# One transformer-like block on a Trainium2 core: small work of VectorE and GpSimd exchanged, S5 inputs in another order, norm sums and reload moved

## The chip, the cores and the metric

The kernel runs on one core of a Trainium2 chip. The metric is the device time of one execution in microseconds, median of several runs. A core has TensorE (matrix products, PE in the profile, its weight loads as PEld), VectorE (DVE), ScalarE (ACT), GpSimd (POOL) and SyncE (SP), which here issues nearly all DMAs. TensorE's clock is granted at one of two levels, 1.2 or 2.4 GHz; the profile gives the granted share as PEclk.

## The reference, cut to what matters

One layer of a hybrid encoder over 2048 prompt tokens and 8 sequences of 16 sample tokens, width 1024, in float32.

```python
h = rmsnorm(x, g);  u = h @ W_in                     # 2828 columns for four head groups
y_a = RG-LRU(conv(u_x)) * gelu(gate)                 # linear recurrence
y_b = SSD(x, B, C, softplus(dt_raw + bias), a)       # chunked state space scan, gated norm
y_c = gated delta rule(l2norm(q), l2norm(k), v, g, beta)
y_d = S5(u_d): complex diagonal states, associative scan, gelu, glu
x += concat(y_a, y_b, y_c, y_d) @ W_out
x += softmax(rmsnorm(x) @ W_q @ K^T / 16) @ V @ W_o  # 256 memory tokens, 4 heads
h = rmsnorm(x);  x += (silu(h @ W_g) * (h @ W_u)) @ W_d   # 2816 hidden columns
y = rmsnorm(x)
```

The states at the end of each recurrence and the memory keys and values are outputs too.

## The kernel before

**Dense work.** Every float32 operand of a dense product is held as two halves, a rounded one (hi) and the rest (lo), and `three` (lines 441 to 443) issues three matmuls for one product. A weight block of 128 x 1024 comes from HBM as `raw`; ScalarE makes its hi half (line 856), VectorE its lo half (line 1040); for blocks that later passes need again, SyncE stores both halves in `kept_dram` (`sp_keep`), and later passes load the halves instead (`sp_kept`, two transfers of 512 KB). There are RAWS 3 raw buffers and SPLITS 4 buffers for the halves. A buffer can be written again when TensorE has used it and its store has landed (`slot_free`). `SPLIT_AHEAD, LOAD_AHEAD, KEPT_AHEAD = 2, 4, 2` (line 36) say how many blocks ahead of its use a block is split, its raw form is loaded, its kept halves are loaded.

**Passes and sections.** Tokens run in six passes of 2, 3, 3, 3, 3 and 3 tiles of 128. All dense work is one ordered list of 787 sections, `SECS`: in a pass `u` and `z` (W_in), `w` (W_out), then attention (`s`, `pt`, `vo` and others), `g`, `up` and `d` (feed-forward), `st` (the sums of squares over the partitions, TensorE line 749) and `final` (scaling and storing the output). The dense results use three PSUM banks in turn. The `st` and the four `final` sections of pass p lie inside the W_in stage of pass p+2, since one pass's mixer overlaps the dense work of another: `st` stands behind the tenth `u` section (`units[9]`). Its input is the running sum `acc` that VectorE builds from ScalarE's squares (line 1049).

**The mixer.** Each of the 17 tiles is a chunk of 21 steps (25 for the sample tile). A generator per engine runs the mixer (`pe_mixer`, `act_mixer`, `dve_mixer`, `pool_mixer`), and `weave` (line 2637) fixes each engine's instruction order: section i, then PLAN[i] steps of the mixer. The plan starts with 16 setup steps and has four steps of token scalars (`dve_scalars`: softplus of dt and of a, on [128, 8 x tiles]) in front of each pass's chunks. An engine works strictly in its order, so a wait holds all that stands behind it.

**Who does what before.** VectorE: lo halves, evictions, convolution taps (line 1131), setup (`dve_setup`, lines 2369 to 2488: exponent, sine arguments, the matrices `bb`, the rotations `rot`), token scalars, scans (line 2073). GpSimd: gate x `rstd` of the feed-forward (line 1270, for every `g` section, 132 times), and in each chunk eight row scalings of the mask `L` (lines 2509 and 2515), three maskings (2520, 2522, 2527) and x times D (2533). TensorE transposes `bb` at setup step 14 (line 1770) and computes the S5 inputs with `pe_bu` (line 1493). SyncE reloads `x` for the next pass in one transfer of 1.5 MB at `u` section 16, once the outputs of the pass before are stored.

Of the kernel before, what the change touches and what calls it, by code (L numbers as in the profile page):

```python
# [14 lines left out]
P = 128  # L15
# [20 lines left out]
SPLIT_AHEAD, LOAD_AHEAD, KEPT_AHEAD = 2, 4, 2  # L36
# [98 lines left out]
def schedule():  # L135
# [108 lines left out]
    for p in range(NP):  # L244
# [20 lines left out]
        if a:  # L265

            units = [s for s in a if s.kind == "u"]
            for k in range(KD):
                units[1 + k].squares = [(fin, k)]
            at = a.index(units[9]) + 1  # L270
            a[at:at] = [st]
            for e, u in zip(end, units[10:]):
                at = a.index(u) + 1
                a[at:at] = [e]
        else:
            for s in last:
                s.squares = [(fin, 2 * s.b), (fin, 2 * s.b + 1)]
            a = [st] + end
# [212 lines left out]
def program(nc, t):  # L491
    ctx = ExitStack()
    with ctx:
# [122 lines left out]
        gs_done, up_done = sem("gs_done"), sem("up_done")  # L616
        out_ready, out_stored = sem("out_ready"), sem("out_stored")
# [518 lines left out]
        def dve_second(eng, i):  # L1136
# [9 lines left out]
            elif unit is not None and unit.cv >= 0:  # L1146
                dve_taps(eng, unit)
            elif s.kind == "up":
# [4 lines left out]
            elif s.kind == "pt":  # L1153
                wide = prompt_at(s.p)[1] * P
                for mt in range(2):
                    slot = s.a % 2 * 2 + mt
                    eng.wait_ge(g_hi_done, s.g + mt + 1)
                    eng.tensor_tensor(g_lo[:, slot, 0:wide], banks[:, (s.f + mt) % 3, 0:wide],
                                      g_hi[:, slot, 0:wide].bitcast(F32), ALU.subtract).then_inc(g_lo_done, 1)
                    eng.drain().then_inc(free[(s.f + mt) % 3], 1)  # L1160
# [26 lines left out]
        def dve_section(eng, i):  # L1187
# [16 lines left out]
            if s.kind == "z" and s.a == 0:  # L1204
                for j in range(tiles(s.p)):
# [4 lines left out]
            elif s.kind == "w":  # L1210
                if s.a == 0:
                    eng.wait_ge(x_loaded, 16 * (s.p + 1))
# [4 lines left out]
            elif scores_at(i) is not None:  # L1217
                s = scores_at(i)
                for j in score_tiles(s):
# [6 lines left out]
                                             ALU.mult).then_inc(s_max, 1)  # L1226
            elif s.kind in ("vo", "so", "d"):
# [22 lines left out]
            elif s.kind == "up":  # L1250
                eng.wait_ge(gs_done, HID * s.p + s.a + 1)
# [10 lines left out]

        def pool_section(eng, i):
            unit = evicted_at(i)
            if unit is not None and unit.kind == "g":
                g = gs[:, unit.a % 2, 0:cols(unit.p)]
                eng.wait_ge(g_gated, unit.ev + 1)
                eng.tensor_tensor(g, g, rstd[:, unit.ni % 2, 0:cols(unit.p)], ALU.mult).then_inc(gs_done, 1)  # L1270
# [103 lines left out]
        def sp_section(eng, i):  # L1374
# [55 lines left out]
            lg=2, dec_m=2, xsd=1)  # L1430
        per_chunk = {k: v if isinstance(v, tuple) else (v, v) for k, v in per_chunk.items()}
        ms = {k: sem("m_" + k) for k in list(per_chunk) + ["in_q", "in_x", "in_l", "in_z", "y_l", "y_x", "y_s", "y_g"]}
        tok_pe, tok_act, tok_dve, tok_exp = sem("tok_pe"), sem("tok_act"), sem("tok_dve"), sem("tok_exp")
        setup_act, setup_dve, setup_pe = sem("setup_act"), sem("setup_dve"), sem("setup_pe")
        state_done = sem("state_done")

        class Chunk:


            def __init__(self, eng, p, c):  # L1440
# [4 lines left out]
                self.ts = tsc[:, p % 2, self.tile, :]  # L1445

# [295 lines left out]
        def pe_scalars(eng, p):  # L1742
# [5 lines left out]
            eng.wait_ge(tok_dve, 2 * p + 2)  # L1748
# [33 lines left out]

        def act_chunk(eng, k):

            k.need("turn", 1)
# [8 lines left out]
            k.need("dec_g")  # L1794
            eng.activation(m["dec"], banks[:, 3, :], ACT.Exp).then_inc(ms["dec_x"], 1)
# [139 lines left out]
        def act_mixer(eng):  # L1935
            for n in range(N_SETUP):
# [41 lines left out]
        def dve_scalars(eng, p):  # L1978
# [7 lines left out]
            eng.scalar_tensor_tensor(na, x8, -1.0, x8, ALU.mult, ALU.min)  # L1986
            eng.drain().then_inc(tok_dve, 1)
# [15 lines left out]
            eng.scalar_tensor_tensor(sp, x8, 0.0, a, ALU.max, ALU.add)  # L2003
# [12 lines left out]
            eng.drain().then_inc(tok_dve, 1)  # L2016
            yield
# [845 lines left out]
```

## Time and profile before

| what | value |
|---|---|
| median of 3 runs | 4240.63 us (4239.75 to 4242.36) |
| the profiled execution | 4238.34 us, of it 4236.5 us span |
| TensorE busy | 3748.2 us, 88% of the span |
| VectorE, ScalarE, GpSimd busy | 2228.1, 1255.2, 320.8 us |
| mean granted TensorE clock | 0.927 |
| DMA | 942 MB, mean 222 GB/s |

How to read it: TensorE is the busiest engine, so what counts is its idle time, 488.3 us in sum, and time at the lower clock. Other engines matter where TensorE waits for them. In the section of rows, a line of a window gives start and end, the length, busy time with the number of instructions for PE, PEld, DVE, ACT and POOL, then PEclk, the DMA share and GB/s. A line of waits gives who waited, for whom, the sum, how often, and the longest. The stages of a pass stand behind each other: W_in (139 us), W_out (37), attention (109) and feed-forward (367) in a middle pass.

### The profile page before, as it was taken

Reading aid. Unit: us, or ns where it says so; the run is one execution under the profiler, and the core shown is the slowest. Engines: PE = TensorE matmul, PEld = TensorE weight load, DVE = VectorE, ACT = ScalarE, POOL = GpSimd, SP = SyncE. Lnnn points to the kernel's source line nnn. Section 1 sums busy time; section 2 is a strip of 40 time slices with the busy share of each in tenths; the row PEclk is TensorE's granted clock in tenths of the full one; section 3 lists DMA queues with packets and bytes.
Section 4 is the critical chain, followed back from the end, with each engine's and each line's share of the span. In section 5 each row is a group of like instructions: output and inputs, shape, how many; then the busy total and the mean of one; then the engine's idle time right before and its main releaser. Section 6 shows DMA issues by size and latency. Waiting matters only on the chain.

```text
span 4236.5 us, 63633 instructions
## 1 busy us (share of the span) xinstructions
PE 3748.2 (88%) x24250; PEld 3627.6 (86%) x24250; DVE 2228.1 (53%) x4752; ACT 1255.2 (30%) x2291; POOL 320.8 (8%) x340
## 2 busy tenths in 40 slices
PE   5587868898788899997899997899998899998998
PEld 5586867798788899997899997899998799998998
DVE  7576644167773545563555554554455455543323
ACT  4344332145432322222323232323232322322101
POOL 0010000001100001100101100001010001100000
PEclk8798977689999999998999998999999999999999
DMA  7755585479968456567555666556666655566776
GB/s 246 239 170 175 175 299 209 130 266 364 350 247 275 163 195 220 206 219 251 191 195 210 220 221 220 208 197 210 212 223 221 216 177 206 199 212 246 244 251 216
DMA packets 372574, 942.08 MB, mean 222 GB/s; under 512 B 35120, under 2 KB 168752, under 8 KB 371760
## 3 DMA queue, kind: packets, MB, share of 16 engines
q1 hardware_dynamic: 372272, 938.03, 63.6%
q8 instruction: 193, 3.16, 0.3%
q14 instruction: 109, 0.89, 0.1%
HBM read 763.32 MB, written 174.57 MB: 221 GB/s over the span
## 4 chain that ended last, share of the span: by engine, by line
PE 54%; DVE 16%; DMA 11%; PEld 6%; DVEq 4%; ACT 3%; issue 3%; SPq 2%; ACTq 0%; PEldq 0%
PE banks L441 15%; PE banks L442 14%; PE banks L443 14%; DMA uc_dram<-uc_sb 3%; DVE m_p_sb L2073 2%; DMA kept_dram<-wlo_sb 2%; DMA wlo_sb<-kept_dram 2%; PEld banks L443 2%; DVE uc_sb L1131 2%; PEld banks L441 2%; PEld banks L442 2%; PE banks L1512 1%; PE banks L1518 1%; DVE wlo_sb L1040 1%; PE banks L1521 1%
## 5 line engine op out<-in xcount | busy, mean ns | idle before, releaser
L441 PE MATMUL banks<-hh_sb,whi_sb 128*128 128x384 f32 (+2 forms) x3552 | 1216.0, 342 | 162.2 <-DVE wlo_sb L1040 58.1
L442 PE MATMUL banks<-hh_sb,wlo_sb 128*128 128x384 f32 (+2 forms) x3552 | 1181.8, 333 | 0.0
L443 PE MATMUL banks<-hl_sb,whi_sb 128*128 128x384 f32 (+2 forms) x3552 | 1180.2, 332 | 0.0
L441 PEld LDWEIGHTS banks<-hh_sb,whi_sb 128*128 128x128 f32 x3552 | 696.6, 196 | 193.1 <-issue 69.1
L442 PEld LDWEIGHTS banks<-hh_sb,wlo_sb 128*128 128x128 f32 x3552 | 697.1, 196 | 2.1 <-issue 1.2
L443 PEld LDWEIGHTS banks<-hl_sb,whi_sb 128*128 128x128 f32 x3552 | 696.0, 196 | 0.0
L441 PE MATMUL banks<-g_hi_sb,whi_sb 128*128 128x384 f32 (+2 forms) x1568 | 541.9, 346 | 77.6 <-DVE g_lo_sb L1151 30.1
L442 PE MATMUL banks<-g_hi_sb,wlo_sb 128*128 128x384 f32 (+2 forms) x1568 | 528.4, 337 | 0.0
L443 PE MATMUL banks<-g_lo_sb,whi_sb 128*128 128x384 f32 (+2 forms) x1568 | 528.3, 337 | 0.0
L441 PEld LDWEIGHTS banks<-g_hi_sb,whi_sb 128*128 128x128 f32 x1568 | 316.5, 202 | 91.2 <-DVE g_lo_sb L1151 33.3
L1232 DVE TENSOR_TENSOR x_sb<-x_sb,banks 128x384 f32<-128x384 f32 (+2 forms) x400 | 202.4, 514 | 330.9 <-PE banks L443 327.4
L441 PE MATMUL banks<-whi_sb,hh_sb 128*128 128x256 f32 (+1 forms) x784 | 246.2, 314 | 108.5 <-DVEq L1160 37.9
L442 PEld LDWEIGHTS banks<-g_hi_sb,wlo_sb 128*128 128x128 f32 x1568 | 317.3, 202 | 0.0
L443 PEld LDWEIGHTS banks<-g_lo_sb,whi_sb 128*128 128x128 f32 x1568 | 316.5, 202 | 0.0
L1023 ACT ACTIVATE g_hi_sb<-gf_sb 128x384 fp32r<-128x384 f32 (+1 forms) x132 | 66.9, 507 | 724.8 <-DVE gf_sb L1253 724.6
L1040 DVE TENSOR_TENSOR wlo_sb<-raw_sb,whi_sb 128x1024 fp32r<-128x1024 f32 (+1 forms) x162 | 199.6, 1235 | 152.4 <-ACT whi_sb L856 150.8
L1270 POOL TENSOR_TENSOR gs_sb<-gs_sb,rstd_sb 128x384 f32<-128x384 f32 (+1 forms) x132 | 129.4, 980 | 1947.9 <-ACT gs_sb L906 1947.9
L441 PEld LDWEIGHTS banks<-whi_sb,hh_sb 128*128 128x128 f32 x784 | 166.3, 212 | 117.9 <-DVEq L1160 39.6
L442 PE MATMUL banks<-whi_sb,hl_sb 128*128 128x256 f32 (+1 forms) x784 | 237.8, 303 | 0.0
L443 PE MATMUL banks<-wlo_sb,hh_sb 128*128 128x256 f32 (+1 forms) x784 | 237.0, 302 | 0.0
L1253 DVE TENSOR_TENSOR gf_sb<-gs_sb,banks 128x384 f32<-128x384 f32 (+1 forms) x132 | 69.8, 529 | 302.4 <-PE banks L443 289.8
L856 ACT ACTIVATE whi_sb<-raw_sb 128x1024 fp32r<-128x1024 f32 (+1 forms) x162 | 169.4, 1051 | 76.0 <-DMA kept_dram<-wlo_sb 62.8
(411 smaller groups left out, 5143.7 us busy)
## 6 DMA issues: line engine op xcount, KB each, us to landing
whi_sb<-kept_dram SPq DMA_DIRECT2D x560, 512.0 KB, 3.7
wlo_sb<-kept_dram SPq DMA_DIRECT2D x560, 512.0 KB, 4.8
raw_sb<-w SPq DMA_DIRECT2D x144, 512.0 KB, 5.0
kept_dram<-whi_sb SPq DMA_DIRECT2D x112, 512.0 KB, 6.5
kept_dram<-wlo_sb SPq DMA_DIRECT2D x112, 512.0 KB, 7.3
uc_dram<-uc_sb SPq DMA_DIRECT2D x90, 192.0 KB, 3.4
ldb_sb<-x_t SPq DMA_DIRECT2D x72, 192.0 KB, 4.6
x_sb<-x_t SPq DMA_DIRECT2D x5, 1536.0 KB, 9.2
```

Of the source, the lines that this page charges most:

```text
L441: eng.matmul(out, xh, yh, start=first, stop=False)
L442: eng.matmul(out, xl, yh, start=False, stop=False)
L443: return eng.matmul(out, xh, yl, start=False, stop=last)
L856: eng.activation(whi[n % SPLITS][:, 0:width], raw[m % RAWS][:, 0:width], ACT.Copy).then_inc(w_hi_done, 1)
L1023: eng.activation(g_hi[:, s.a - sum(BLOCKS[:s.b]), 0:n], gf[:, s.a % 2, 0:n], ACT.Copy).then_inc(g_hi_done, 1)
L1040: eng.tensor_tensor(wlo[n % SPLITS][:, 0:width], raw[m % RAWS][:, 0:width], whi[n % SPLITS][:, 0:width].bitcast(F32), ALU.subtract).then_i ...
L1131: last = eng.scalar_tensor_tensor(out[:, 0:n], u[:, tap:tap + n], wc, out[:, 0:n], ALU.mult, ALU.add)
L1232: eng.tensor_tensor(out, out, bank[:, 0:wide], ALU.add).then_inc(free[(s.f + dd) % 3], 1)
L1253: eng.tensor_tensor(gf[:, s.a % 2, 0:n], gs[:, s.a % 2, 0:n], bank[:, 0:n], ALU.mult).then_inc(up_done, 1)
L1270: eng.tensor_tensor(g, g, rstd[:, unit.ni % 2, 0:cols(unit.p)], ALU.mult).then_inc(gs_done, 1)
L1512: last = eng.matmul(banks[:, 3, h * P:h * P + P], head("decs", h, P), head("ST1", h, P), start=True, stop=True)
L2073: eng.tensor_tensor_scan(dst[:, s * P:s * P + P], mag[:, n:n + 1].to_broadcast([P, P]), src[:, s * P:s * P + P], s5_x[:, part, n:n + 1], A ...
```

## The change

- Setup and the whole token softplus run on GpSimd alone, without being woven in (`setup`, `scalars`); only reciprocals stay on VectorE. Operations with three operands are written as two. `yield`s fall away. The other engines wait for `setup_pool` counts; SyncE, ScalarE and VectorE wait for 5, the end of the setup, before the first chunk.
- The gate x `rstd` product goes to VectorE, the mask rows to ScalarE (`act_rows`, eight per chunk), the maskings and x times D to VectorE. The strict mask falls away.
- `pe_bu` issues the two halves of the partitions in turn instead of one after the other.
- `st` stands two `u` sections later, and each `final` as well.
- VectorE evicts `pt` after its squares and taps; PLAN is 0 at these sections.
- `x` is reloaded in quarters at `u` 16, `u` 17, `z` 0 and `z` 1.
- SPLIT_AHEAD goes from 2 to 3 and LOAD_AHEAD from 4 to 5.

```diff
-SPLIT_AHEAD, LOAD_AHEAD, KEPT_AHEAD = 2, 4, 2
+SPLIT_AHEAD, LOAD_AHEAD, KEPT_AHEAD = 3, 5, 2
...
-            at = a.index(units[9]) + 1
+            at = a.index(units[11]) + 1
             a[at:at] = [st]
-            for e, u in zip(end, units[10:]):
+            for e, u in zip(end, units[12:]):
...
+            elif unit is not None and unit.kind == "g":
+                g = gs[:, unit.a % 2, 0:n]
+                eng.wait_ge(g_gated, unit.ev + 1)
+                eng.tensor_tensor(g, g, rstd[:, unit.ni % 2, 0:n], ALU.mult)
+                eng.drain()
...
             elif s.kind == "up":
-                eng.wait_ge(gs_done, HID * s.p + s.a + 1)
...
-            if s.kind == "u" and s.b == 16 and s.p >= 2:
-                sp_x(eng, s.p - 1)
+            if s.p >= 2 and (s.kind == "u" and s.b >= 16 or s.kind == "z"):
+                sp_x(eng, s.p - 1, s.b - 16 if s.kind == "u" else 2 + s.a)
...
-            for half, bank in enumerate((bank_a, bank_b)):
-                r = slice(half * 64, half * 64 + 64)
-                for part in range(2):
-                    for u in range(2):
-                        o = part * 256 + u * P
+            for part in range(2):
+                for u in range(2):
+                    o = part * 256 + u * P
+                    for half, bank in enumerate((bank_a, bank_b)):
+                        r = slice(half * 64, half * 64 + 64)
                         eng.matmul(banks[:, bank, o:o + P], bbt[r, part, j, u, :], in_l[r, 4 + j, :], start=True, stop=True)
...
                 if n == N_SETUP - 2:
-                    eng.wait_ge(setup_dve, 3)
+                    eng.wait_ge(setup_pool, 4)
...
+        def act_rows(eng, k, first):
+            for h in range(4):
+                eng.activation(lg[:, h, :], k.later, ACT.Copy, scale=k.ts[:, G8 + first + h:G8 + first + h + 1])
+            eng.drain().then_inc(ms["lg"], 1)
         def act_chunk(eng, k):
+            k.before("ws")
+            act_rows(eng, k, 4)
             k.need("turn", 1)
...
             k.need("dec_g")
+            act_rows(eng, k, 0)
             eng.activation(m["dec"], banks[:, 3, :], ACT.Exp).then_inc(ms["dec_x"], 1)
...
-            tt(by_pair(m["decs"]), kq[:, 0], by_pair(m["decs"]), ALU.mult)
-            tt(by_pair(m["dec"]), kq[:, 1], by_pair(m["dec"]), ALU.mult)
+            tt(by_pair(m["decs"]), kq[:, 0], by_pair(m["dec"]), ALU.mult)
...
+            tt(by_pair(m["dec"]), kq[:, 1], by_pair(m["dec"]), ALU.mult)
...
+            tt(m["xsd"], m["tx"][:, 0:256], mc("ssd_d"), ALU.mult)
+            tt(dec, dec, k.upto.unsqueeze(1).to_broadcast([P, 4, P]), ALU.mult)
+            k.need("dec_x", 2)
+            tt(dcs, dcs, k.upto.unsqueeze(1).to_broadcast([P, 4, P]), ALU.mult)
...
         def dve_mixer(eng):
-            yield from dve_setup(eng)
-            for p in range(NP):
-                yield from dve_scalars(eng, p)
-                if p == 0:
-                    eng.wait_ge(sample_in, 16 * 4)
-                yield from chunks(eng, p, dve_chunk)
+            for n in range(N_SETUP):
+                if n == 3:
+                    eng.wait_ge(setup_pool, 3)
+                    eng.reciprocal(sw[8][:], sw[8][:])
+                    eng.reciprocal(sm[:, 6:8], sm[:, 6:8])
+                    eng.drain().then_inc(setup_inv, 1)
+                yield
+            for p in range(NP):
+                yield
+                eng.wait_ge(tok_den, p + 1)
+                z = tk[:, 5, 0:tiles(p) * 8]
+                eng.reciprocal(z, z).then_inc(tok_inv, 1)
+                yield
+                yield
+                eng.wait_ge(tok_exp, p + 1)
+                yield
+                if p == 0:
+                    eng.wait_ge(setup_pool, 5)
+                    eng.wait_ge(sample_in, 16 * 4)
+                yield from chunks(eng, p, dve_chunk)
...
         def pool_mixer(eng):
-            for _ in range(N_SETUP):
-                yield
+            for _ in setup(eng):
+                pass
+            eng.drain().then_inc(setup_pool, 1)
             for p in range(NP):
+                eng.wait_ge(r12_done, PASSES[p][1])
+                if p:
+                    eng.wait_ge(tok_pe, p)
+                    eng.wait_ge(ms["upd"], PASSES[p - 1][0])
+                scalars(eng, p)
```

## Rows read from the trace of the kernel before

**Rows 1.** The page: busy us by engine; stores of kept halves
```profile
PE 3748.2 (88%) x24250; PEld 3627.6 (86%) x24250; DVE 2228.1 (53%) x4752; ACT 1255.2 (30%) x2291; POOL 320.8 (8%) x340
...
kept_dram<-wlo_sb SPq DMA_DIRECT2D x112, 512.0 KB, 7.3
```

**Rows 2.** By window: us, then busy (x) of PE, PEld, DVE, ACT, POOL
```profile
19.00:166.00 147.00, 94.21 (x550) 88.62 (x550) 105.20 (x369) 61.29 (x105) 0.00 (x0) 0.83 0.75 247
592.00:878.00 286.00, 236.68 (x1284) 210.88 (x1285) 105.19 (x218) 73.27 (x136) 9.06 (x8) 0.67 0.54 185
878.00:1197.00 319.00, 267.61 (x2188) 259.65 (x2188) 229.57 (x398) 151.35 (x226) 39.09 (x46) 0.94 0.93 347
1854.00:1993.00 139.00, 117.58 (x731) 114.17 (x731) 75.27 (x162) 40.22 (x72) 0.00 (x0) 0.93 0.69 236
2139.00:2506.00 367.00, 355.92 (x2276) 349.56 (x2275) 187.30 (x361) 93.14 (x171) 44.32 (x46) 0.98 0.60 207
3940.00:4237.00 297.00, 279.96 (x1592) 277.73 (x1590) 79.35 (x137) 34.38 (x61) 22.30 (x22) 0.97 0.69 237
```

**Rows 3.** Waits: engine, line <- releaser: total us, times, longest
```profile
ACT whi_sb L856 <- DMA kept_dram<-wlo_sb: 62.8, 31, 6.7
...
PE banks L441 <- DVE wlo_sb L1040: 67.2, 24, 7.2
PE banks L441 <- DMA wlo_sb<-kept_dram: 52.1, 21, 6.6
DVE uc_sb L1095 <- DMA uc_dram<-uc_sb: 88.5, 19, 8.0
PE banks L749 <- DVE acc_sb L1049: 33.0, 6, 7.2
```

**Rows 4.** Timeline: start, us, engine, line, operation, shape, count
```profile
123.44 1.91 PE L1770 MATMUL banks<-mixc_sb,bb_sb 128*128 128x128 f32 x16
```

**Rows 5.** By shape: count | busy, mean ns; DVE until 165 us
```profile
L1270 POOL TENSOR_TENSOR gs_sb<-gs_sb,rstd_sb 128x384 f32<-128x384 f32 x110 | 112.6, 1024 | 1563.4 <-ACT gs_sb L906 1563.4
L2509 POOL TENSOR_SCALAR m_lg_sb<-mixc_sb,tsc_sb 128x128 f32<-128x128 f32 x64 | 40.6, 653 | 1004.4 <-DVEq L2016 931.0 <-PE banks L1483 73.4
L2856 POOL MEMSET const-float32-0.0<- 128x1 f32 x1 | 0.1, 99 | 0.2 <-issue 0.2
...
L2358 DVE TENSOR_TENSOR ex_sb<-ex_sb 128x8 f32<-128x8 f32 x16 | 2.7, 167 | 1.2
L2463 DVE TENSOR_TENSOR bt_sb<-sw_sb,s5b_sb 128x1024 f32<-128x1024 f32 x1 | 1.2, 1221 | 0.0
...
L1846 ACT ACTIVATE m_yo_sb<-banks,tsc_sb 128x64 f32<-128x64 f32 x68 | 15.8, 315 | 53.9 <-PE banks L1612 53.5 <-PE banks L1483 0.5
```

**Rows 6.** Chain by line, 880 to 1190 us, then 1850 to 1960
```profile
by line: DMA kept_dram<-wlo_sb 12.0%; PE banks L441 7.9%; PE banks L443 7.1%; PE banks L442 7.0%; ACT whi_sb L856 6.4%; DVE wlo_sb L1040 6.4%; DVEq L1254 4.9%; DVE m_p_sb L2073 4.5%; issue 4.4%; DVEq L1089 3.2%; DMA ldb_sb<-x_t 2.7%; DVE m_
...
by line: DMA uc_dram<-uc_sb 17.9%; DVE uc_sb L1131 12.3%; DMA wlo_sb<-kept_dram 4.9%; PE banks L441 4.8%; PE banks L442 4.3%; PE banks L443 4.3%; issue 4.0%; DVE acc_sb L1049 3.1%; ACT uc_sb L924 2.6%; DVE m_p_sb L2073 2.5%; PEld banks L442
```

**Rows 7.** Timeline around the norm sums L749, [idle before <- releaser]
```profile
1905.68 0.34 PE L443 MATMUL banks<-hl_sb,whi_sb 128*128 128x384 f32 x1
1912.49 1.65 PE L749 MATMUL banks<-acc_sb,ones_sb 128*128 128x384 f32 x2 [6.48 <-DVE acc_sb L1049]
...
1911.88 0.56 DVE L1049 TENSOR_TENSOR acc_sb<-acc_sb,sqb_sb 128x384 f32<-128x384 f32 x1
...
1967.46 0.59 PE L441 MATMUL banks<-whi_sb,hh_sb 128*128 128x268 f32 x1 [4.76 <-DMA wlo_sb<-kept_dram]
```

**Rows 8.** timeline of 1600 to 1612 us: DVE, GpSimd, TensorE
```profile
1602.71 5.11 DVE L2073 TENSOR_TENSOR_SCAN m_p_sb<-mag_sb,s_x_sb,m_p_sb 128x128 f32<-128x128 f32 x8
...
1601.03 3.62 POOL L2515 TENSOR_SCALAR m_lg_sb<-mixc_sb,tsc_sb 128x128 f32<-128x128 f32 x4
...
1604.47 0.34 PE L443 MATMUL banks<-g_lo_sb,whi_sb 128*128 128x384 f32 x1
1608.32 0.69 PE L441 MATMUL banks<-g_hi_sb,whi_sb 128*128 128x384 f32 x1 [3.52 <-DVE x_sb L1232]
1608.81 0.52 PE L442 MATMUL banks<-g_hi_sb,wlo_sb 128*128 128x384 f32 x1
```

**Rows 9.** timeline, the same scans with GpSimd idle
```profile
1888.85 3.12 DVE L2073 TENSOR_TENSOR_SCAN m_p_sb<-mag_sb,s_x_sb,m_p_sb 128x128 f32<-128x128 f32 x8
```

**Rows 10.** timeline, two blocks of 16 matmuls with 64 rows in each operand
```profile
1591.24 1.71 PE L1493 MATMUL banks<-m_in_l_sb,bbt_sb 64*128 64x128 f32 x16
...
243.15 1.16 PE L1564 MATMUL banks<-m_cht_sb 64*128 64x128 f32 x16 [0.28 <-ACT m_cht_sb L1800]
```

More of the change, by code:

```diff
@@ L615, in program @@
         s_max, s_exp, p_done = sem("s_max"), sem("s_exp"), sem("p_done")
-        gs_done, up_done = sem("gs_done"), sem("up_done")
-        out_ready, out_stored = sem("out_ready"), sem("out_stored")
+        up_done = sem("up_done")
+        out_ready, out_stored = sem("out_ready"), [sem(f"out_stored{q}") for q in range(KD // 2)]
         qs_done, ps_done, pst_done = sem("qs_done"), sem("ps_done"), sem("pst_done")
@@ L1152, in dve_second @@
                                   ALU.subtract).then_inc(g_lo_done, 1)
[L1153 to L1160, printed above, removed]
             elif s.kind == "sv":
@@ L1226, in dve_section @@
                                              ALU.mult).then_inc(s_max, 1)
+            elif s.kind == "pt":
+                wide = prompt_at(s.p)[1] * P
+                for mt in range(2):
+                    slot = s.a % 2 * 2 + mt
+                    eng.wait_ge(g_hi_done, s.g + mt + 1)
+                    eng.tensor_tensor(g_lo[:, slot, 0:wide], banks[:, (s.f + mt) % 3, 0:wide],
+                                      g_hi[:, slot, 0:wide].bitcast(F32), ALU.subtract).then_inc(g_lo_done, 1)
+                    eng.drain().then_inc(free[(s.f + mt) % 3], 1)
             elif s.kind in ("vo", "so", "d"):
@@ L1445, in __init__ @@
                 self.ts = tsc[:, p % 2, self.tile, :]
+                self.upto = sc("Us") if self.sample else mc("U")
+                self.later = sc("Ls") if self.sample else mc("L")
             def base(self, name):
@@ L2002, in dve_scalars @@
             eng.drain()
-            eng.scalar_tensor_tensor(sp, x8, 0.0, a, ALU.max, ALU.add)
+            eng.tensor_scalar(sp, sp, 0.5, None, ALU.mult)
+            eng.drain()
+            eng.tensor_tensor(sp, sp, a, ALU.add)
             eng.drain()
@@ L2173, in dve_chunk @@
             k.need("kq")
-            k.need("dec_m", 1)
+            k.need("dec_x", 1)
             def by_pair(ap):
@@ L2238, in dve_chunk @@
             k.need("yo")
-            k.need("xsd")
             k.loaded("in_z")
@@ L2376, in dve_setup @@
             eng.drain()
-            tt(w_t1, are, w_step, ALU.mult).then_inc(setup_dve, 1)
+            tt(w_t1, are, w_step, ALU.mult).then_inc(setup_pool, 1)
             yield
@@ L2385, in dve_setup @@
             eng.drain()
-            stt(w_r, w_k, -TWO_PI_HI, w_ang, ALU.mult, ALU.add)
-            eng.drain()
-            stt(w_r, w_k, -TWO_PI_MID, w_r, ALU.mult, ALU.add)
-            eng.drain()
-            stt(w_r, w_k, -float(TWO_PI_LO), w_r, ALU.mult, ALU.add)
-            eng.drain().then_inc(setup_dve, 1)
+            for part, src in ((TWO_PI_HI, w_ang), (TWO_PI_MID, w_r), (float(TWO_PI_LO), w_r)):
+                ts(w_t2, w_k, -part, None, ALU.mult)
+                eng.drain()
+                tt(w_r, src, w_t2, ALU.add)
+                eng.drain()
+            eng.drain().then_inc(setup_pool, 1)
             yield
@@ L2397, in dve_setup @@
             tt(w_den, w_t2, w_t3, ALU.add)
-            eng.drain()
-            eng.reciprocal(w_den, w_den)
             eng.wait_ge(setup_act, 1)
@@ L2402, in dve_setup @@
             ts(z, e, 2.0, None, ALU.add)
-            eng.drain()
-            eng.reciprocal(z, z)
-            eng.drain()
+            eng.drain().then_inc(setup_pool, 1)
+            eng.wait_ge(setup_inv, 1)
             tt(z, z, e, ALU.mult)
@@ L2415, in dve_setup @@
             eng.drain()
-            stt(sm[:, 0:2], a, 2.0, sm[:, 0:2], ALU.mult, ALU.add)
+            ts(a, a, 2.0, None, ALU.mult)
+            eng.drain()
+            tt(sm[:, 0:2], sm[:, 0:2], a, ALU.add)
             eng.drain()
@@ L2468, in dve_setup @@
             tt(bb[:, 1], bb[:, 1], t3, ALU.add)
-            eng.drain().then_inc(setup_dve, 1)
+            eng.drain().then_inc(setup_pool, 1)
             cos, sin = rot[:, 0], rot[:, 1]
@@ L2692, in _ @@
             sp.wait_ge(finals_stored, 16 * len(outs))
-            sp.wait_ge(out_stored, 16 * KD * NP)
+            for stored_pair in out_stored:
+                sp.wait_ge(stored_pair, 32 * NP)
             sp.wait_ge(sample_stored, 16 * 5)
```

127 lines of the change are left out of this document (49 added, 78 removed).

## The prediction

> **What bounds the kernel now.** I read the engines' busy times first. TensorE is busy 3748 of 4236.5 us [rows 1], so at most 488 us of idle time and the time at the lower clock can be had; no removed instruction counts unless TensorE waits for it. The windows tell which stage has the idle time [rows 2]. In the steady feed-forward TensorE is busy 355.9 of 367 us, in the last one 280.0 of 297: little is left. A steady W_in stage has 21 of 139 us idle, the first one 53 of 147, and pass 0's attention and feed-forward 49 of 286 and 51 of 319. Then the waits name the releaser [rows 3]: in pass 0 the lo halves and, behind them, stores of kept halves; in the W_in stages VectorE's running sum (33.0 us in six waits), the loads of kept halves and the stores of convolution outputs. Last, the timeline shows what a gap costs besides itself: ahead of the 3.52 us gap at 1604.8 a matmul takes 0.34 us, behind it 0.52 [rows 8], the lower of the clock's two levels. Across the trace a gap of 3.5 us or more is followed by about 6.8 us of such matmuls, in which half the work gets done: up to 3.4 us more.
>
> **Part by part.** The profiled execution is 4238.3 us (span 4236.5 and 1.8 around it), 2.3 under the median. I sum differences against it and apply them to the median.
>
> *Setup off VectorE.* Some 104 instructions on 128x8 cost 0.167 us and a drain of 1.2/16 = 0.075, together 25 us; six on 128x1024 at 1.22 make 7.3 [rows 5]; with the rotations, VectorE loses about 40 of its 105.2 us in the first window [rows 2]. TensorE is busy 94 of 147 there, so the gain lies between 0 and 40. The DMA share is 0.75 and the chain raw, hi, lo, kept store remains, so I take well under half: **−15**. On GpSimd the same work is not in the trace. The nearest rows are 0.65 us for a scaling of 128x128 and 0.10 for a memset of 128x1 [rows 5]; small operations lie between. At 0.35 to 0.9 us, 114 of them to `bb`, with six wide ones at about 2.4 (a 128x384 product takes 1.02), need 54 to 117 us from 12 us on, so `bb` is ready at 66 to 129; before, TensorE reads it at 123.4 [rows 4]. The rotations follow by about 182 at the latest; SyncE's first mixer step stands near 170. Hidden in my case.
>
> *Token softplus on GpSimd.* 26 operations in a row at 0.35 to 0.9 are 9 to 23 us, against 5 on VectorE. It is hidden in passes 1 to 4, where 18 us or more lie between VectorE's last scalar and TensorE's read. Passes 0 and 5 have 4.2 and 1.1 us: **+10** (0 to +25). The shorter VectorE queues behind the first stage return **−5**.
>
> A product of 128x384 takes GpSimd 1.02 us [rows 5] and VectorE 0.56 [rows 7]. The Trainium skill, "GPSIMD Engine Reference", section 4.1, sends elementwise work to VectorE, GpSimd being about twice slower with two inputs; the pair of rows agrees, at 1.8. It speaks against this move, and as an estimate by it the 26 operations would take 10 us in place of 5, so +5 in place of +10 and −62 as the whole sum.
>
> *Splitting three ahead with four buffers.* The split of block n needs the store of block n−4 landed. That store stands on SyncE behind a raw load that waits for the lo half of block n−2 (n−3 before). So two blocks now go round a loop of hi and lo (about 3 us) and a store of 7.3 [rows 1]: 5.15 us a block, where three did before (3.4). Pass 0's feed-forward has 68 blocks in 319 us [rows 2], 4.7 each. If the loop binds, that is 0.45 x 68 = +31. Against it, TensorE waits 67.2 us for lo halves and ScalarE 62.8 for kept stores [rows 3]; an earlier split can save some of the first, and I take −20 of 67.2. The kept store is already the largest entry of the chain there, 12.0% [rows 6]. Net **+12** (−30 to +60).
>
> *Norm sums two units later.* TensorE ends at 1906.0 and waits 6.48 us for a sum that VectorE delivers at 1912.4 [rows 7], and then runs at half speed. Two units later VectorE has had about 7 us more for it. Gap and clock are about 10 us, but the W_in stage's chain is led by the stores of convolution outputs, 17.9%, and VectorE's taps, 12.3% [rows 6], which don't move: late next are the loads at `z` 0 (4.76 us [rows 7]), and the finals now land nearer to the reload. I keep **−6** in each of four stages (0 to −10), **−24**. Reloading in quarters is put at 0 (−3 to +3 a pass): the last quarter is issued behind `z` 1 and is due at the first W_out eviction some 5 us after.
>
> *Mask rows to ScalarE, masks to VectorE.* A row scaling of 128x64 takes ScalarE 0.315 us [rows 5]; eight of 128x128 are about 3 us a chunk, in an engine busy 93 of 367 and 39 of 109 us. VectorE gets two maskings, x times D and `decs` from PSUM as before: about 1.8 us a chunk, busy 187 of 367 [rows 2]. In the attention stages, where steps are doubled, rows and waits cost 1.5 a pass and GpSimd's absence returns 2: with a gain at the bank waits **−5** in all.
>
> *GpSimd out of VectorE's way.* Eight scans take 5.11 us while GpSimd scales rows [rows 8], and 3.12 when it is idle [rows 9]. In the first case an eviction waits behind them, and TensorE for the eviction, 3.52 us and the clock after it. Without the 2.0 us the gap is at 1.5. Two such gaps a pass, each 2 to 3 us and up to 3.4 of clock. The new work on VectorE is 22 gate products at 0.55 and a drain per pass, 14 us spread over 367 with 180 idle. The gate's product was awaited only now and then before. Over four feed-forward stages I take **−17** (−40 to +10); the last stage has an idle VectorE and gives 0.
>
> *S5 inputs in turn.* The same 16 matmuls take 1.71 us half after half and 1.16 where halves alternate (L1564) [rows 10]: 0.55 less. 17 chunks have two blocks, 34 x 0.55 = 18.7; most chunks stand where TensorE is the bound, the rest beside other waits: **−13** (−19 to 0).
>
> Sum: −15 + 10 − 5 + 12 − 24 − 5 − 17 − 13 = **−57**, which makes 4240.6 − 57 = **4184**.
>
> **Rivals.** (a) *The kept-store loop decides pass 0.* If stores land in 9.5 us because the DMA share is 0.93 [rows 2], the loop takes (3 + 9.5)/2 = 6.25 us a block, 1.55 x 68 = +105 in place of +31: 4184 + 74 = **4258**, slower. It decides against the change once a block takes 6.0 us, a store 9.0. For it: the store leads the chain there, and the deeper split makes ScalarE, with its evictions behind, wait for a younger store. Against: 7.3 is the median at just this load. (b) *GpSimd's chain is late.* If a small operation takes over 1.0 us, `bb` and the rotations end after 123 and 182, and SyncE, with all weight loads behind it, waits: 4184 + 35 = **4219**. For it: no small operation is in the trace; against: 0.10 for the memset. The Trainium skill, "GPSIMD Engine Reference", section 2.1, has every GpSimd instruction pass two steps, a broadcast and a dispatcher in software, the latter at tens of cycles; by that the fixed cost is far from 1 us and (b) would not come. No row of the trace before can show it. (c) *Gains given back.* The W_in stages are held by the convolution stores, the wait only moves to the loads at `z` 0, and VectorE's added products eat the relief; then A0 −15, tokens +10, S5 −10, loop +12 and little more remain: **4236**, no change. (d) *More than I take*: every sum gap and its clock (−40), both feed-forward gaps (−40), loop never binding (−20): **4125**. (e) That `pe_bu` alternates without overlapping costs 13 of the gain and stays in the forecast's range.
>
> **How the numbers follow.** Forecast (4155 to 4215) 0.50; (d) 0.10; (a) 0.15; (b) 0.10; (c) 0.15. A measurement tells about 0.2%, 8.5 us, from no change, so the border is at 4232 and 4249. Faster: 0.50 + 0.10 + 0.10 + 0.03 of (c) = 0.73. Same: 0.10 of (c). Slower: 0.15 + 0.02 = 0.17. The range reaches to (d) and over most of the loop's bound, 4125 to 4250; it leaves out most of (a) and the tail of (d).
>
> **What would show it.** In the changed profile: DVE busy in the first window near 65 and TensorE's read of `bb` not later than 123; no wait of SyncE or DVE for the setup's end; ScalarE's wait for kept stores in pass 0 above 62.8 if the loop binds, well above 100 for (a); the L749 waits under 10 us in sum; eight scans at 3.1 us everywhere; L1493 blocks at 1.16; feed-forward stages of 359 to 364 us. I am wrong if W_in stages stay at 139 us with the gap only renamed, if pass 0's feed-forward is over 340 us, or if small operations of GpSimd take over 1 us.

## The result

The changed kernel takes **4275.6 us** (median of 4, 4273.7 to 4279.3) against 4240.2 before: 1.008 of the time, 95% interval 1.0065 to 1.0094. It is slower by 35 us where the forecast had 57 us less. The profiled execution has a span of 4272.0 us. The page of the changed kernel, busy times and stores:

```profile
PE 3722.4 (87%) x24250; PEld 3600.0 (84%) x24250; DVE 2212.3 (52%) x4605; ACT 1296.7 (30%) x2423; POOL 122.6 (3%) x354
...
kept_dram<-wlo_sb SPq DMA_DIRECT2D x112, 512.0 KB, 7.0
```

TensorE is busy 26 us less than in [rows 1] and idle 61 us more. Where the time went shows when the span is cut at the first dense matmul of each stage, and the lengths are subtracted (us):

| stages | before | changed | difference |
|---|---|---|---|
| W_in of pass 0 (it begins 1.0 us later, not counted here) | 147.5 | 158.2 | +10.7 |
| memory K and V | 199.3 | 201.4 | +2.1 |
| W_in of pass 1 | 180.3 | 184.7 | +4.4 |
| W_out, attention of pass 0 | 332.4 | 345.5 | +13.1 |
| feed-forward of pass 0 | 318.3 | 376.0 | +57.7 |
| W_in of passes 2 to 5 | 560.8 | 544.0 | −16.8 |
| W_out of passes 1 to 5 | 194.4 | 199.8 | +5.4 |
| attention of passes 1 to 5 | 519.2 | 506.3 | −12.9 |
| feed-forward of passes 1 to 4 | 1469.2 | 1440.1 | −29.1 |
| feed-forward of pass 5 | 296.1 | 295.9 | −0.2 |

So up to the end of pass 0's feed-forward, where all weights are split, the change costs 89 us (with the 1.0 of the start), and behind it it gains 54, about what the forecast had for that part. The windows of the changed kernel for the stages of [rows 2]: first W_in, attention and feed-forward of pass 0, then W_in and feed-forward of a middle pass.

```profile
20.00:178.00 158.00, 93.67 (x550) 88.32 (x551) 90.26 (x215) 62.09 (x106) 64.50 (x151) 0.79 0.75 252
...
615.00:910.00 295.00, 227.57 (x1287) 202.78 (x1288) 104.91 (x223) 77.27 (x148) 2.17 (x9) 0.69 0.54 177
910.00:1286.00 376.00, 284.20 (x2185) 273.31 (x2184) 232.95 (x424) 157.18 (x239) 0.00 (x0) 0.88 0.85 292
1927.00:2062.00 135.00, 114.07 (x730) 110.24 (x730) 74.04 (x159) 38.52 (x71) 0.77 (x3) 0.96 0.69 237
...
2205.00:2564.00 359.00, 351.00 (x2280) 344.20 (x2278) 192.45 (x388) 98.09 (x187) 0.00 (x0) 1.00 0.62 211
```

The line of 910 to 1286 us is the one that matters: VectorE and ScalarE do nearly the same work as before (233 against 230 us and 157 against 151), TensorE's 2185 matmuls take 17 us longer at a granted clock of 0.88 where it was 0.94, and the DMA share fell from 0.93 to 0.85, while the stage is 57 us longer. So the engines wait. The waits, as in [rows 3]:

```profile
DVE wlo_sb L1040 <- ACT whi_sb L856: 288.6, 110, 14.2
...
ACT whi_sb L856 <- DMA kept_dram<-wlo_sb: 186.0, 66, 10.5
...
PE banks L441 <- DVE wlo_sb L1040: 7.1, 5, 2.8
PE banks L749 <- DVE acc_sb L1049: 7.0, 2, 4.9
```

TensorE's direct wait for lo halves is gone (67.2 to 7.1) and so is the wait for the norm sums (33.0 to 7.0). ScalarE's wait for the kept stores has tripled (62.8 to 186.0), and VectorE's for the hi halves has nearly doubled with it (150.8 to 288.6). The chain that ended last in 912 to 1280 us, by line (in [rows 6] the store had 12.0%):

```profile
by line: DMA kept_dram<-wlo_sb 42.8%; DVE wlo_sb L1040 12.0%; ACT whi_sb L856 8.1%; SPq L1283 4.5%; issue 2.9%; SPq L1302 2.9%; DVE m_p_sb L2083 2.3%; PE banks L441 2.1%; PE banks L443 1.9%; DMA wlo_sb<-kept_dram 1.9%; PE banks L442 1.8%; D
```

And one round of it, in the timelines of VectorE, SyncE and ScalarE:

```profile
965.71 1.23 DVE L1040 TENSOR_TENSOR wlo_sb<-raw_sb,whi_sb 128x1024 fp32r<-128x1024 f32 x1 [3.25 <-ACT whi_sb L856]
...
966.97 0.33 SPq L1302 DMA_DIRECT2D raw_sb<-w  x1
967.34 0.43 SPq L1283 DMA_DIRECT2D kept_dram<-whi_sb  x1
967.82 0.43 SPq L1283 DMA_DIRECT2D kept_dram<-wlo_sb  x1
971.85 0.33 SPq L1302 DMA_DIRECT2D raw_sb<-w  x1
...
974.77 1.06 ACT L856 ACTIVATE whi_sb<-raw_sb 128x1024 fp32r<-128x1024 f32 x1 [4.21 <-DMA kept_dram<-wlo_sb]
...
975.86 1.23 DVE L1040 TENSOR_TENSOR wlo_sb<-raw_sb,whi_sb 128x1024 fp32r<-128x1024 f32 x1 [3.38 <-ACT whi_sb L856]
...
977.12 0.33 SPq L1302 DMA_DIRECT2D raw_sb<-w  x1
```

A lo half ends at 966.94; SyncE's raw load (L1302) goes at once, since it waited for it, and only then the store (L1283), 967.34 and 967.82. ScalarE, waiting for that store, starts the next hi half at 974.77; the lo half follows, and at 977.12 SyncE is released again. That is 10.15 us for a round, with one other block in between (raw load at 971.85): 5.1 us a block. The stage needs 376/68 = 5.5, and needed 4.7 before. Over the whole stage, the starts of a hi half and of the second one behind it are 10.9 us apart in the median, and half of these distances lie between 10.3 and 12.0.

### The profile page after: what moved, and what is told of

The parts are those of the page before. It is cut to its first block, busy times and chain, and to the rows that moved or that the text cites. A ratio compares the mean times of both kernels' runs of the same rounds, so it can differ in the third digit from the quotient of the medians.

```text
span 4272.0 us, 63638 instructions
## 1 busy us (share of the span) xinstructions
PE 3722.4 (87%) x24250; PEld 3600.0 (84%) x24250; DVE 2212.3 (52%) x4605; ACT 1296.7 (30%) x2423; POOL 122.6 (3%) x354
## 4 chain that ended last, share of the span: by engine, by line
PE 48%; issue 19%; DVE 11%; DMA 10%; ACT 4%; DVEq 2%; SPq 2%; POOLq 1%; POOL 1%; ACTq 1%; PEld 0%; PEldq 0%
PE banks L441 13%; PE banks L443 13%; PE banks L442 13%; DMA kept_dram<-wlo_sb 5%; DVE wlo_sb L1040 2%; DMA wlo_sb<-kept_dram 2%; PE banks L1518 1%; DVE uc_sb L1131 1%; PE banks L1512 1%; ACT whi_sb L856 1%; PE banks L1521 1%; PE banks L804 1%; DVE m_p_sb L2083 1%; DMA uc_dram<-uc_sb 1%; DMA x_sb<-k_cache_t 1%
## 5 line engine op out<-in xcount | busy, mean ns | idle before, releaser
L441 PE MATMUL banks<-hh_sb,whi_sb 128*128 128x384 f32 (+2 forms) x3552 | 1213.2, 342 | 148.8 <-DVE hl_sb L1057 43.9
L1040 DVE TENSOR_TENSOR wlo_sb<-raw_sb,whi_sb 128x1024 fp32r<-128x1024 f32 (+1 forms) x162 | 201.2, 1244 | 289.9 <-ACT whi_sb L856 288.6
L856 ACT ACTIVATE whi_sb<-raw_sb 128x1024 fp32r<-128x1024 f32 (+1 forms) x162 | 170.7, 1055 | 223.0 <-DMA kept_dram<-wlo_sb 186.0
L906 ACT ACTIVATE gs_sb<-gs_sb 128x384 f32<-128x384 f32 (+1 forms) x132 | 66.9, 506 | 386.4 <-DVE gs_sb L1088 386.4
```

Of the source, the lines that this page charges most:

```text
L441: eng.matmul(out, xh, yh, start=first, stop=False)
L856: eng.activation(whi[n % SPLITS][:, 0:width], raw[m % RAWS][:, 0:width], ACT.Copy).then_inc(w_hi_done, 1)
L906: eng.activation(out, out, ACT.Silu).then_inc(g_gated, 1)
L1040: eng.tensor_tensor(wlo[n % SPLITS][:, 0:width], raw[m % RAWS][:, 0:width], whi[n % SPLITS][:, 0:width].bitcast(F32), ALU.subtract).then_i ...
```

## The experiments

Times in one group share the chip and the runs of the kernel before; ratios are to those runs. Theory A: SyncE's raw load, which waits for a lo half, stands ahead of the store, and with 3 and 5 two blocks share a round. Theory B: the deeper split alone is at fault. Theory C: other parts of the change cost pass 0. A stage time is read from one trace of each run, cut as above.

**The two constants.** One line each: in the changed kernel 2/4, 3/4 and 2/5 for SPLIT_AHEAD/LOAD_AHEAD, and 3/5 in the kernel before.

```diff
-SPLIT_AHEAD, LOAD_AHEAD, KEPT_AHEAD = 3, 5, 2
+SPLIT_AHEAD, LOAD_AHEAD, KEPT_AHEAD = 2, 4, 2
```

> The changed kernel with SPLIT_AHEAD 2 and LOAD_AHEAD 4 as before. Theory A: the two constants close a ring of two blocks (lo half of block n-2, SyncE's store of block n-4, hi half of block n) and cost pass 0 alone; the feed-forward of pass 0 goes from 376 back to about 318 us, and with some 15 us more from the other stages of pass 0 the kernel takes 4195 to 4210 us, under the kernel before (4240). Theory C: the other parts (setup on GpSimd, its waits, gates on VectorE) cost pass 0; then the feed-forward stage stays over 350 and the kernel over 4255.

> The changed kernel with SPLIT_AHEAD 3 and LOAD_AHEAD 4. Theory A: SyncE's raw load then waits for the lo half of one block earlier, so its store of block n-4 goes out after the lo half of block n-3: three blocks share one round of 10.3 us, 3.4 each, and the ring doesn't bind; feed-forward of pass 0 at 315 to 330 us, kernel at 4195 to 4215. Theory B: it is the deeper split alone, ScalarE waiting one block earlier for a younger store; the stage stays over 350 us and the kernel over 4240.

> The changed kernel with SPLIT_AHEAD 2 and LOAD_AHEAD 5. Theory A: SyncE's raw load waits for the lo half of block n-2 before it stores block n-4, as in the change, so two blocks share a round of 10.3 us or more: feed-forward of pass 0 over 350 us, kernel at 4245 to 4290. Theory B: the shallow split heals it; 4195 to 4215.

> The kernel before with SPLIT_AHEAD 3 and LOAD_AHEAD 5 and nothing else. Theory A: pass 0 pays as in the change, its feed-forward over 365 us, and the kernel takes 4300 to 4330 us, since nothing of the later gains is there. Theory C: about 4240, as before.

| run | time | ratio, interval | first W_in | feed-forward of pass 0 |
|---|---|---|---|---|
| e1, changed, 2/4 | 4184.9 | 0.9873 (0.9856 to 0.9889) | 149.5 | 323.4 |
| e2, changed, 3/4 | 4157.4 | 0.9811 (0.9796 to 0.9825) | 133.8 | 326.7 |
| e3, changed, 2/5 | 4387.3 | 1.0350 (1.0331 to 1.0368) | 233.7 | 375.6 |
| e4, before, 3/5 | 4327.3 | 1.0213 (1.0196 to 1.0230) | 157.7 | 378.3 |

C falls: without the constants the change is 53 us faster than before, and the constants alone make the kernel before 89 us slower. B falls: the split three ahead with a load four ahead is the best of the four. A load five ahead gives 376 to 378 us in the feed-forward, whatever the split. The times themselves were missed three times: 2/4 and 3/4 came 10 and 38 us under their ranges, and for 2/5 I had 4245 to 4290 and it takes 4387. Its first stage is 84 us longer than with 2/4, where SyncE's convolution stores and token loads stand behind the same wait. One row speaks for it: ScalarE waits 95.3 us for the convolution stores (line 920), all in the first 250 us, and 16.4 us in the whole run with 2/4. How that wait closes is argued, not shown.

```profile
ACT uc_sb L920 <- DMA uc_dram<-uc_sb: 95.3, 12, 9.6
```

**The order on SyncE.** Constants 3 and 5 stay; a section's stores are issued ahead of its raw load (and of loads of kept halves, which pass 0 doesn't have).

```diff
+            for n in range(before, s.after):
+                if W_KEPT[n] >= 0:
+                    sp_keep(eng, n)
             sp_weights(eng, min(N_W, before + LOAD_AHEAD) if i else RAWS, ...)
...
-            for n in range(before, s.after):
-                if W_KEPT[n] >= 0:
-                    sp_keep(eng, n)
```

> The changed kernel with 3 and 5 as it is; SyncE only issues a section's kept stores ahead of its raw load instead of behind it. Theory A: the store of block n-4 then waits for the lo half of block n-3 and no longer for n-2, three blocks share a round, and the ring is gone with both constants in place: feed-forward of pass 0 at 320 to 332 us, kernel at 4150 to 4175 us. Rival: it is the number of buffers against the depth of 5 itself; the stage stays over 350 us and the kernel over 4240.

4178.5 us, ratio 0.9853 (0.9837 to 0.9869), 3 us over the range for the kernel; the feed-forward of pass 0 takes 327.8 us, as expected. The wait in question, 186.0 in the changed kernel:

```profile
ACT whi_sb L856 <- DMA kept_dram<-wlo_sb: 36.1, 21, 5.6
```

Three moved lines give back 97 us. The mechanism is thus the store's place behind the raw load's wait, neither the depth of 5 nor the four buffers as such. By stage, the moved lines give 19.4 us in the first W_in (158.2 to 138.8), 20.6 in W_out and attention of pass 0 (345.5 to 324.9), 48.2 in the feed-forward, and under 1 us in each of the K and V stage and W_in of pass 1.

**Setup and splits together.** The kernel before with 3/4 alone.

> The kernel before with SPLIT_AHEAD 3 and LOAD_AHEAD 4 alone. In the changed kernel these constants gave 27.6 us against 2 and 4. If an earlier split helps by itself, the kernel before gains the same, about 4210 us, with its first stage at 132 to 136 us. If the gain needs VectorE freed of the setup (38 us of its 122 in that stage), the stage stays over 143 us and the kernel over 4225.

4230.1 us, ratio 0.9972 (0.9960 to 0.9985). The first stage takes 148.8 us. With the setup moved and 2/4 it was 149.5; with both it is 133.8. Each alone gains nothing there. In the run with 2/4 TensorE waits for lo halves, as in the kernel before (45.2 us there); in the kernel before with 3/4 it waits for VectorE's evictions instead. The two waits in the first 153 us, of the run with 2/4 and of this one:

```profile
PE banks L441 <- DVE wlo_sb L1040: 44.2, 13, 7.1
```

```profile
PE banks L441 <- DVEq L1113: 31.9, 11, 6.8
```

TensorE's weight loads (PEld) wait for lo halves in both, 44.4 and 38.9 us, and 21.9 with both changes (e2). So the two limits lie close together.

**Parts undone, on the changed kernel with 2/4.** The norm sums at the tenth unit (`units[9]`, `units[10:]`); `pe_bu` half after half; the gate products on GpSimd, pass by pass, with VectorE's `up` waiting for them; `x` reloaded whole at unit 16.

> As e1 (changed kernel, 2 and 4: 4184.9 us) with the norm sums behind the tenth unit again, as before. Theory: the gain of the W_in stages of passes 2 to 5 (143.8, 139.0, 139.0, 139.0 us before, 138.9, 135.3, 136.2, 136.6 in e1) is that of the moved sums; they return to about 143, 139, 139, 139 and the kernel takes 4196 to 4204 us. Rival: the gain comes from VectorE's shorter queue or the reload in quarters; then the kernel stays at 4182 to 4190.

4204.3 us, 0.991 (0.988 to 0.9941). The interval touches that of 2/4; the stages decide: W_in of passes 2 to 5 sum to 558.8 us against 547.0, **11.8 us** for the two units. In the nine traces that have the sums at the twelfth unit and the reload in quarters this sum lies between 543.3 and 547.8, so a difference of 4 us could not be told from that spread, and 11.8 can.

> As e1 with the S5 inputs issued half after half. Theory: a block of 16 takes 1.7 in place of 1.2 us, 34 blocks, most of them on the path: 4194 to 4204 us. Rival: the alternation hides nothing on the path: 4182 to 4188.

4195.5 us, 0.9901 (0.9872 to 0.993), 10.6 us above 2/4 by the medians, which this interval can't confirm. The blocks themselves are clear: in the changed kernel one takes 1.16 us where [rows 10] has 1.71, and all of them 43.1 where they were 60.7:

```profile
1672.19 1.16 PE L1493 MATMUL banks<-m_in_l_sb,bbt_sb 64*128 64x128 f32 x16
...
L1493 PE MATMUL banks<-m_in_l_sb,bbt_sb 64*128 64x128 f32 x544 | 43.1, 302 | 0.0
```

The same line in the kernel before:

```profile
L1493 PE MATMUL banks<-m_in_l_sb,bbt_sb 64*128 64x128 f32 x544 | 60.7, 293 | 0.0
```

> As e1 with the gate products of the feed-forward on GpSimd again (132 of about 1.02 us) and off VectorE. Theory: it was the row scalings and maskings, long and in bursts, that slowed VectorE's scans, not the gate product; the middle feed-forward stages stay at 358 to 361 us and the kernel at 4180 to 4195. Rival: the gate product carries the gain of these stages (367 to 359); then they go back over 363 and the kernel to 4205 or more.

4189.7 us, 0.9878 (0.9856 to 0.99): the same as without. The middle feed-forward stages are at 358.5, 359.2 and 358.2 us. The gate product's engine makes no difference that these runs can tell.

> As e1 with x reloaded in one go at the seventeenth unit as before. Put at 0 in the prediction. If the quarters ease the loads at the first z section, the W_in stages of passes 2 to 5 get longer by 1 to 2 us each and the ratio is 0.988 to 0.990; if not, 0.987.

4203.0 us, 0.9908 (0.9893 to 0.9923). W_in of passes 2 to 5: 554.3 us against 547.0. The reload in quarters, which I had put at nothing, is worth 7.3 us in these stages (4 to 8 had been expected before this run), and the ratio is just over the expected range. The wait for the kept loads, 44.4 us with quarters, is 55.1 here (52.1 in [rows 3]):

```profile
PE banks L441 <- DMA wlo_sb<-kept_dram: 55.1, 22, 5.9
```

**Mask rows.** Base 2/4; GpSimd runs the eight scalings per chunk again, not woven in.

```diff
-            act_rows(eng, k, 4)
...
-            act_rows(eng, k, 0)
...
                 scalars(eng, p)
+                for c in range(*PASSES[p]):
+                    k = Chunk(eng, p, c)
+                    k.before("ws")
+                    rows(eng, k, 4)
+                    k.need("dec_g")
+                    rows(eng, k, 0)
```

> As e1 (changed kernel, 2 and 4, 0.987 of before) with the eight mask rows of each chunk on GpSimd again. Theory: bursts of GpSimd rows slow VectorE's scans and with them an eviction; scans beside them go from 3.1 to about 5 us for eight, the middle feed-forward stages from 359 back to 362 to 365 us, and the kernel takes 0.990 to 0.994 of before. Rival: the gain of these stages comes from VectorE's new order of the masks alone; then they stay under 360 us and the ratio at 0.987 to 0.989.

4169.7 us, **0.9833** (0.9819 to 0.9848): faster than with the rows on ScalarE, on the other side of both expectations. The middle feed-forward stages are at 355.7, 356.3 and 355.5. The mean scan takes 0.464 us, against 0.587 before, with rows on GpSimd both times. Of the 256 scans of this run 40 lie mostly beside a row scaling and take 0.481 us in the mean, and 206 beside nothing take 0.461. So the rows hardly slowed them. The trace of the kernel before tells what did, once the burst of [rows 8] is cut: scans until 1604.7 and from 1604.95 us, by shape, and GpSimd's maskings beside the latter. Ahead of them stand all scans of this run and all of the kernel before:

```profile
L2080 DVE TENSOR_TENSOR_SCAN m_p_sb<-mag_sb,s_x_sb,m_p_sb 128x128 f32<-128x128 f32 x256 | 100.4, 464 | 2.9 <-issue 0.4
...
L2073 DVE TENSOR_TENSOR_SCAN m_p_sb<-mag_sb,s_x_sb,m_p_sb 128x128 f32<-128x128 f32 x256 | 132.4, 587 | 2.6
...
L2073 DVE TENSOR_TENSOR_SCAN m_p_sb<-mag_sb,s_x_sb,m_p_sb 128x128 f32<-128x128 f32 x6 | 2.4, 462 | 0.1
...
L2073 DVE TENSOR_TENSOR_SCAN m_p_sb<-mag_sb,s_x_sb,m_p_sb 128x128 f32<-128x128 f32 x3 | 3.2, 1119 | 0.0
...
1604.83 1.30 POOL L2520 TENSOR_TENSOR m_dec_sb<-m_dec_sb,mixc_sb 128x512 f32<-128x512 f32 x1 [0.18 <-issue]
1606.28 1.26 POOL L2522 TENSOR_TENSOR m_decs_sb<-m_dec_sb,mixc_sb 128x512 f32<-128x512 f32 x1
```

Over the whole trace 61 scans lie mostly beside row scalings (L2515) and take 0.473 us in the mean, 146 beside nothing take 0.460, 17 mostly beside masking L2520 take 1.30 in the mean and 15 beside L2522 take 1.50. The scaling reads one tensor, the masking two and is longer.

**Tokens on VectorE, and sums later still,** both on 3/4 (0.9811).

> As e2 (changed kernel, 3 and 4, 0.981 of before) with the token softplus on VectorE again and only the setup on GpSimd. Theory: GpSimd's chain is some 5 us longer and is late in the last pass and perhaps the first; W_out of pass 4 goes from 45.8 back to 38 to 40 us, the rest stays within 3 us, and the ratio is 0.979 to 0.981. Rival: the chain's place is hidden elsewhere and VectorE's longer queue costs as much; 0.981 to 0.983.

4165.8 us, 0.9826 (0.9807 to 0.9846): no difference in the whole. W_out of pass 4 goes from 45.8 to 38.2 us as expected; where the whole loses it again is open, VectorE's longer queue being the likely place. In the changed kernel that stage shows GpSimd's chain being late, a wait that the kernel before doesn't have:

```profile
3375.31 0.62 PE L1752 MATMUL banks<-tmp_sb,mixc_sb 128*128 128x24 f32 x2 [2.82 <-POOLq L2030]
```

> As e2 with the norm sums behind the fourteenth unit and the final sections behind the last four. From tenth to twelfth the four stages gained 11.8 us. If VectorE's running sum is still late at the twelfth, another 4 to 10 us (ratio 0.978 to 0.980); if the rest is the stores and loads at the stage's end, the finals now meet them and it is 0.981 to 0.985.

4152.7 us, 0.9797 (0.9781 to 0.9813), W_in of passes 2 to 5 at 532.6 us against 544.0: another 11.4 us in the stages, of which the medians of the whole show 4.7, within their noise.

**Together.** 3/4, sums at the fourteenth unit, rows on GpSimd; and the same with 3/5 and the stores first.

> The changed kernel with 3 and 4, the norm sums at the fourteenth unit and the mask rows on GpSimd. If the gains add, 4152 (e11) less about 13 (e9 against e1): 4135 to 4145 us. If the rows on ScalarE cost only where the shallow split held ScalarE, 4148 to 4158.

> As e14 with 3 and 5 and the stores ahead of the raw loads. If a raw load one block earlier is worth anything once the ring is gone, 3 to 15 us under e14; if raw loads are early enough at 4, the same within 5 us.

**4131.9 us**, ratio 0.974 (0.9725 to 0.9754), and 4153.6 us, 0.9788 (0.9772 to 0.9805). The first beats the kernel before of its own group (4242.4) by 110 us and the changed kernel by 144. It came 3 us under the range expected for gains that add. The second is 22 us slower than the first, where the same or less was expected. Most of it is in the K and V stage (198.8 against 183.6 us), as with e13 against e2 (200.7 against 186.9). The changed kernel too has 201.4 us there, with 3/5 and the stores behind the raw load, and 201.0 with 2/4: of its variants only those with 3/4 are short in this stage. Why is open.

## Why the prediction was wrong

**Splitting three ahead** is the step that failed: the term stood at +12, and the two constants measured +89 us in the kernel before (e4) and +91 in the changed one (4275.6 against 4184.9, from two groups). That is 77 to 79 of the 92 us between the forecast and the time; all other terms together stood at −69 and measured −53 (e1). The ring was described rightly (two blocks in a round of 10.3 us; the trace has 10.15), and it was priced at +31 for the feed-forward, −20 for lo waits saved, nothing elsewhere. Three sizes were off. The saved lo waits were no gain while the ring binds; TensorE's wait for lo halves went, and ScalarE's wait for the stores came in its place. The pace in the feed-forward was 5.5 us a block and not 5.15, +58: 10.3 us is the shorter end of the rounds and not their mean. That other work of ScalarE and VectorE lands in the longer ones is likely, and no run shows it. And the ring binds outside the feed-forward too, in the first W_in and in W_out and attention of pass 0: 40 us, by what moving the stores gave back there (e13). The ring comes from the load five ahead (e3), and not from the split for which the term is named: with the load at four, three ahead gains 28 us (e2 against e1). Rival (a), slower, came true by its mechanism, at 0.15 and 4258; I wanted a store of 9.0 us for it, and it came with a median of 7.0. The range ended at 4250.

**Setup off VectorE** (−15) gave nothing by itself: the first stage takes 149.5 us with 2/4 and took 147.5. With 3/4 it takes 133.8, against 148.8 in the kernel before with 3/4 (e5), just 15.0 less. So the gain needs the earlier split with it. VectorE's busy time fell by 15 us in the window and not by 40, 105.2 to 90.3. Part of the 40 were drains, which don't count as busy, and what stays got 17 us longer beside GpSimd's setup: the convolution taps of lines 1128 and 1129, the lo halves, and two copies. The changed kernel until 178 us, then the kernel before until 166:

```profile
L1129 DVE SCALAR_TENSOR_TENSOR uc_sb<-ust_sb,par_sb,uc_sb 128x128 f32<-128x128 f32 x42 | 20.0, 477 | 0.0
...
L1108 DVE COPY ust_sb<-stail_sb 128x24 f32<-128x24 f32 x14 | 6.4, 455 | 0.1
...
L1110 DVE TENSOR_TENSOR ust_sb<-banks,rstd_sb 128x128 f32<-128x128 f32 x14 | 3.9, 278 | 0.0
...
L1129 DVE SCALAR_TENSOR_TENSOR uc_sb<-ust_sb,par_sb,uc_sb 128x128 f32<-128x128 f32 x42 | 14.5, 345 | 0.0
...
L1108 DVE COPY ust_sb<-stail_sb 128x24 f32<-128x24 f32 x14 | 2.4, 173 | 0.1
```

GpSimd was in time: `bb` is ready by 98 us, since most small operations take 0.20 to 0.35 us and only single ones about 1; rival (b) fell. The −5 for VectorE's shorter queues behind the first stage doesn't show: the K and V stage and W_in of pass 1 take 380.1 us with 2/4 and took 379.6.

**Token softplus** (+10): +6 in the last pass (W_out of pass 4, 38.2 to 44.3), and e10 shows nothing in the whole.

**Norm sums** (−24): 11.8 measured, half, but **reload in quarters** (0) gives 7.3. The loads at `z` 0 were late next as said (2.90 and 2.79 us at 2031.8 and 2036.3, where [rows 7] has 4.76). Together 16.8 gained in the changed kernel; in these stages the sum matmuls no longer wait:

```profile
1994.07 0.81 PE L749 MATMUL banks<-acc_sb,ones_sb 128*128 128x384 f32 x2
...
2031.77 0.36 PE L441 MATMUL banks<-whi_sb,hh_sb 128*128 128x268 f32 x1 [2.90 <-DMA wlo_sb<-kept_dram]
```

**GpSimd out of VectorE's way and the S5 order** (−17 and −13): 29.1 in four feed-forward stages and 12.9 in the attention stages, more than counted. Of the S5 order alone e7 has 10.6, which its interval can't confirm. The gap of 3.5 us [rows 8] is 2.20 in the changed kernel, and the granted clock of a middle stage went from 0.98 to 1.00:

```profile
2326.10 0.44 PE L441 MATMUL banks<-g_hi_sb,whi_sb 128*128 128x384 f32 x1 [2.20 <-DVE x_sb L1239]
```

The effect was right, its cause was not: I blamed the row scalings, and it was the maskings. **Mask rows to ScalarE**, in a term of −5, cost some 15 us of the gain (e9).

The forecast of 4184 is nearly what the change without its constants takes (4184.9). That is luck: without its +12 the sum was 4172, and behind it quarters and feed-forward gave more than put, setup, mask rows and sums less.

Two slips in the working change nothing in this. The matmuls behind a gap of 3.5 us or more don't run for 6.8 us at the lower clock: most of the stretches granted 0.5 are 6.8 us long, but they begin within the gap, and the matmuls behind it have mostly 2.9 to 5.8 us of them, at 1608.3 us 5.5. That makes 1.5 to 2.9 us lost and not up to 3.4. And (d) leaves out that the loop's +12 goes too: its terms make 4113 and not 4125.

## What to carry to other kernels

Before a pipeline is made deeper, write down the ring through the buffers: what frees a buffer, in whose queue that step stands, and which wait stands ahead of it there; the number of blocks in the ring divides its round. If the pace comes out slower than the present one, the waits it saves elsewhere are not to be counted against it, and the round is the least that a block can take, not the mean. Put what frees a buffer ahead of what only fetches early: here three lines on the DMA queue were worth 97 us.

## What the runs showed of the hardware

- A 128x128 scan on VectorE takes 0.460 us alone, 0.473 in the mean of 61 beside a GpSimd scaling with one tensor input, and 1.3 to 1.5 beside a masking with two, which itself takes 1.30 and 1.26. The Trainium skill, "GPSIMD Engine Reference", section 1, names contention where VectorE has two SBUF inputs or is in a 2-port mode; these rows add that it matters what GpSimd runs. Its number of inputs is the likely reason; shape and operation differ too (128x128 scaling, 128x512 product), and no run changed one of them alone.
- What VectorE reads matters too. In the first stage its operations on SBUF got longer beside GpSimd's setup (taps of line 1129 0.345 to 0.477 us, copies of line 1108 0.173 to 0.455), while its evictions from PSUM kept their time (line 1110, 0.282 and 0.278).
- Both sides pay. GpSimd's 128x8 operations take 0.20 us with VectorE idle; later in the setup line 2377 has a mean of 0.312, from single ones near 1 us. VectorE's lo halves have a mean of 1.38 us in that stage, where they took 1.22:

```profile
15.36 0.20 POOL L2379 TENSOR_SCALAR ex_sb<-ex_sb 128x8 f32<-128x8 f32 x1 [0.16 <-issue]
15.71 0.20 POOL L2377 TENSOR_TENSOR ex_sb<-ex_sb 128x8 f32<-128x8 f32 x1
...
17.24 0.99 POOL L2377 TENSOR_TENSOR ex_sb<-ex_sb 128x8 f32<-128x8 f32 x1
...
L1040 DVE TENSOR_TENSOR wlo_sb<-raw_sb,whi_sb 128x1024 fp32r<-128x1024 f32 x20 | 27.6, 1380 | 31.0 <-ACT whi_sb L856 31.0
```

- A one-input scaling of 128x128 takes GpSimd 0.65 to 0.92 us and ScalarE 0.39; it was still better on GpSimd (e9), in whose trace no engine is seen waiting for the rows.
